# Building the expert gate table by GpSimd scatter-adds instead of one-hot products on TensorE

## The reference

```
q  = (xn @ w_pq) -> 8 heads x 2 halves x 128
s1, s2 = q @ sub_k1, q @ sub_k2            # 128 keys each
v1,i1 = top_k(s1,16); v2,i2 = top_k(s2,16) # per token and head
vs,ci = top_k(v1[:,None]+v2[None,:], 16)   # 16 of 256 pairs
e1, e2 = i1[ci // 16], i2[ci % 16]
expert = e1 * 128 + e2                     # one of 16384
gate   = softmax(vs)
out[t] = sum_k gate[t,k] * gelu(u[expert[t,k]] . xn[t]) * v[expert[t,k]]
```

## Time and profile before

| | us |
|---|---|
| median of 3 runs | 3006.87 (3006.38 to 3007.98) |
| the profiled execution | 3007.15 |
| its span, first to last instruction | 3005.4 |
| PE busy | 2962.8 (99%) |
| DVE busy | 2020.9 (67%) |
| ACT busy | 1488.6 (50%) |
| POOL busy | 169.0 (6%) |

### The profile page before, as it was taken

The page is one execution under the profiler, slowest core; times in us unless marked ns, Lnnn a source line. Parts: engine busy times, 40 slices in busy tenths (PEclk is TensorE's granted clock), DMA queues, the critical chain, the costliest instruction groups (busy, mean ns, idle before and its releaser), DMA issues.

```text
span 3005.4 us, 42961 instructions
## 1 busy us (share of the span) xinstructions
PE 2962.8 (99%) x17085; PEld 2678.9 (89%) x17085; DVE 2020.9 (67%) x2869; ACT 1488.6 (50%) x2274; POOL 169.0 (6%) x312
## 2 busy tenths in 40 slices
PE   8999999999999999999999999999999999999999
PEld 7998778888888888978789999999999999999999
DVE  5656654444445445554557988888888888888876
ACT  4355544444444444454444466447745555555553
POOL 2000000000000002140000000000010000000000
PEclk9999999999999999999999999999999999999999
DMA  7554355556554554535667779778999899899764
GB/s 255 160 169 154 114 169 193 189 188 193 184 195 182 194 189 150 169 109 208 190 208 249 237 261 338 238 222 293 337 371 360 300 328 321 310 322 318 264 221 141
DMA packets 238382, 690.73 MB, mean 230 GB/s; under 512 B 14249, under 2 KB 95177, under 8 KB 203392
## 3 DMA queue, kind: packets, MB, share of 16 engines
q1 hardware_dynamic: 221024, 598.71, 59.2%
q0 software_dynamic: 12608, 71.73, 6.3%
q10 hardware_dynamic: 4576, 17.89, 1.6%
HBM read 652.61 MB, written 33.57 MB: 228 GB/s over the span
## 4 chain that ended last, share of the span: by engine, by line
PE 51%; DVE 0%; ACTq 0%; ACT 0%; issue 0%; DVEq 0%
PE banks L2156 16%; PE banks L2232 14%; PE banks L2157 8%; PE banks L2233 7%; PE banks L2203 2%; PE banks L2253 1%; PE banks L2255 1%; PE banks L2254 1%; PE banks L2175 0%; DVE peer_features L378 0%; DVE weights_lo L195 0%; PE banks L2192 0%; PE banks L2221 0%; ACTq L2310 0%; DVE residual L2585 0%; DVE peer_scratch L2584 0%
## 5 line engine op out<-in xcount | busy, mean ns | idle before, releaser
L195 DVE TENSOR_TENSOR weights_lo<-weights,weights_hi 128x1024 fp32r<-128x1024 f32 (+4 forms) x1080 | 1228.5, 1179 | 701.8 <-ACT weights_hi L188 700.0
L188 ACT ACTIVATE weights_hi<-weights 128x1024 fp32r<-128x1024 f32 (+4 forms) x1080 | 1046.4, 1017 | 1316.8 <-PE banks L419 640.8
L2156 PE MATMUL banks<-peer_features,weights_hi 128*128 128x448 f32 (+1 forms) x2304 | 738.9, 377 | 2.7 <-DVE weights_lo L195 2.7
L417 PE MATMUL banks<-weights_hi,features_hi 128*128 128x512 f32 (+3 forms) x1600 | 605.2, 378 | 12.5 <-DVE weights_lo L195 9.3
L2157 PE MATMUL banks<-peer_features,weights_lo 128*128 128x224 f32 (+1 forms) x2304 | 615.3, 267 | 0.0
L419 PE MATMUL banks<-weights_hi,features_lo 128*128 128x512 f32 (+3 forms) x1600 | 600.5, 375 | 0.0
L418 PE MATMUL banks<-weights_lo,features_hi 128*128 128x512 f32 (+3 forms) x1600 | 600.4, 375 | 0.0
L2232 PE MATMUL banks<-peer_features,weights_hi 128*128 128x448 f32 x1568 | 492.4, 374 | 0.0
L2156 PEld LDWEIGHTS banks<-peer_features,weights_hi 128*128 128x128 f32 x2304 | 432.0, 187 | 44.2 <-DVE weights_lo L195 3.2
L2157 PEld LDWEIGHTS banks<-peer_features,weights_lo 128*128 128x128 f32 x2304 | 438.6, 190 | 0.0
L2233 PE MATMUL banks<-peer_features,weights_lo 128*128 128x224 f32 x1568 | 414.3, 264 | 0.0
(11 more groups left out here) (406 smaller groups left out, 2757.7 us busy)
## 6 DMA issues: line engine op xcount, KB each, us to landing
weights<-in_expert_u SPq DMA_DIRECT2D x128, 1024.0 KB, 5.5
weights<-in_expert_v SPq DMA_DIRECT2D x128, 1024.0 KB, 7.2
weights<-in_w_ffn_gate SPq DMA_DIRECT2D x44, 1024.0 KB, 5.1
weights<-in_w_ffn_up SPq DMA_DIRECT2D x44, 1024.0 KB, 5.1
weights<-in_w_ffn_down SPq DMA_DIRECT2D x44, 1024.0 KB, 4.8
weights<-in_w_in SPq DMA_DIRECT2D x48, 900.0 KB, 4.7
weights<-in_w_out SPq DMA_DIRECT2D x32, 1024.0 KB, 5.1
weights<-in_w_in SPq DMA_DIRECT2D x24, 704.0 KB, 4.2
```

The source lines that it names most:

```text
L188: act.activation(hi[:, k, n], raw[:, k, n], ACT.Copy).then_inc(self.hi_ready, 1 + skip)
L195: last = dve.tensor_tensor(lo[:, k, n], raw[:, k, n], hi[:, k, n].bitcast(F32), ALU.subtract)
L417: pe.matmul(out, xh, wh, start=first, stop=False)
L2156: pe.matmul(self.bank(n % 3, 2 * (T - lo)), wh[:, k, :], F[:, k, :, lo:T], start=(k == 0), stop=False)
```

## The change

1. PE's one-hot products, the transposes for them and all work of ACT and DVE for them are gone. `expert_gates` is laid out `(key, expert, token)`, is set to zero by 16 POOL DMAs of 896 KB in the feed-forward of block 1, and is filled by 256 indirect DMAs of POOL that add: each takes one slot (of 128) for all tokens of a tile, 96 or 128 values of 4 bytes, each to its own cell. DVE works out the cell numbers (two small operations a part). At the first slot of each head (every 16) POOL waits until all scatters before have landed, since two heads can name one cell.
2. The 32 row tokens are now the last 32 of the last tile, so that tile is chosen first: `RET` is (44, 10), choosing runs from step 10 to 43 and 44 to 77. The score products stand four steps ahead of each part (`SCORE`).
3. POOL's order is fixed: 160 scatters (`early`), with row gathers 0 to 2 behind the first three; then row gather c, four scatters, row gather c+1, four scatters and so on, until the scatters run out behind gather 26. Each scatter of a part waits for that part's gates (`chosen`), each gather for its buffer (`row_summed`).
4. `SUM` is now 78 to 125 without multiples of 6, 126 to 141, 143 to 150.
5. From step 2 to 271 `weights_lo` is one operation of 128x2048, that starts when both halves of `weights_hi` are there.
6. SP waits for all 256 scatters where it waited for the stored gates. The `expert_gates` loads are contiguous.

```diff
+    def split_lo_whole(self, dve, stream, i, j, half):
+        hi, lo, raw = ...
+        dve.wait_ge(self.hi_ready, i * 16 + (2 * (2 * (self.fills + j) + half) + 2))
+        dve.tensor_tensor(lo, raw, hi.bitcast(F32), ALU.subtract).then_inc(self.lo_ready, 1)
...
+                        self.pool_chain.on(pool)(pool.memset(zeros[:, :], 0.0))
+                        parts = NKEYS // self.ZEROED
+                        for n in range(parts):
+                            pool.wait_ge(ring.used, ring.done(1 + n // 2, 4 * (n % 2)))
+                            pool.dma_start(self.g_d[:, self.ZEROED * n:self.ZEROED * (n + 1), :],
+                                           zeros[:, :].rearrange("p (e t) -> p e t", e=self.ZEROED)).then_inc(self.gates_zeroed, 16)
...
-        SC, RET, TURN = 18, (22, 74), (55, 107)
-        HOT = [(58 + i, 0, ROWS // 8 + i) for i in range(16 - ROWS // 8)] + [(110 + i, 1, i) for i in range(16)]
-        SUM = [56, 57, *range(58, 74), *range(108, 142), *range(V0 - 1, V0 + 8), *range(V0 + 9, V0 + 12)]
+        FIRST, RET = NT - 1, (44, 10)
+        SUM = [s for s in range(78, 126) if s % 6] + [*range(126, 142), *range(V0 - 1, V0 + 7)]
+        SCORE = [RET[(FIRST + q // 4) % NT] + 8 * (q % 4) - 4 for q in range(4 * NT)]
...
+                    ch(dve.tensor_scalar(vif[:, 0:2, :].rearrange("p h k -> p (h k)"), eg[:, 0, slots], float(DENSE), token[:, t:t + 1],
+                                         ALU.mult, ALU.add))
+                    ch(dve.scalar_tensor_tensor(out=cell_of[:, t, slots], in0=eg[:, 1, slots], scalar=float(NKEYS * DENSE),
+                                                in1=vif[:, 0:2, :].rearrange("p h k -> p (h k)"), op0=ALU.mult, op1=ALU.add))
...
-                                for b in range(2):
-                                    sp.wait_ge(gates_out[b], 8 * BLKS)
-                                sp.wait_ge(gated, DENSE // 4)
+                                sp.wait_ge(scattered, 16 * NT * SLOTS)
...
+                    def scatter(n):
+                        t, slot = (FIRST + n // SLOTS) % NT, n % SLOTS
+                        tokens = P - ROWS if t == FIRST else P
+                        if slot % TOPK == 0:
+                            pool.wait_ge(chosen, n // (HP * TOPK) + 1)
+                            if slot > 0:
+                                pool.wait_ge(scattered, 16 * n)
+                        pool.indirect_dma_start(out=g_rows[:, :], in_=gates_of[0:tokens, t, slot:slot + 1], in_offset=None,
+                                                compute_op=ALU.add,
+                                                out_offset=bass.IndirectOffsetOnAxis(ap=cell_of[0:tokens, t, slot:slot + 1], axis=0))\
+                            .then_inc(scattered, 16)
+                    pool.wait_ge(zeroed, 16 * NKEYS // self.ZEROED)
+                    early, mixed = SLOTS + HP * TOPK, 4
+                    for n in range(early):
+                        scatter(n)
+                        if n < BUFS:
+                            gather(n)
+                    for c in range(BUFS, 2 * ROWS):
+                        gather(c)
+                        for n in range(early + mixed * (c - BUFS), min(early + mixed * (c - BUFS + 1), NT * SLOTS)):
+                            scatter(n)
...
-                        for t, r, place_in_order in hot_step(n):
-                            for g in (2 * r, 2 * r + 1):
...
-                                for c in range(4):
-                                    last = pe.matmul(self.bank(3 + g % 2, P, c * P), h[:, 0, c, :], h[:, 1, c, :],
-                                                     start=True, stop=True)
...
-                        ring.split_lo(dve, tiles, i, j, half)
+                        if s < 2:
+                            ring.split_lo(dve, tiles, i, j, half)
+                        else:
+                            ring.split_lo_whole(dve, tiles, i, j, half)
```

More of the change, by code:

```diff
@@ L196, in split_lo @@
         last.then_inc(self.lo_ready, 1 + skip)
+    def split_lo_whole(self, dve, stream, i, j, half):
+        hi, lo, raw = self.piece(self.hi, half, stream), self.piece(self.lo, half, stream), self.raw(j, half, stream)
+        dve.wait_ge(self.hi_ready, i * 16 + (2 * (2 * (self.fills + j) + half) + 2))
+        dve.tensor_tensor(lo, raw, hi.bitcast(F32), ALU.subtract).then_inc(self.lo_ready, 1)
     def wait(self, pe, i, j, half):
@@ L1927, in peer @@
             skT = scratch[:, 4096:6144].rearrange("p (j n) -> p j n", j=PQ_TILES)
-            gblk = scratch[:, 0:4096].rearrange("p (b e t) -> p b e t", b=2, t=BLK)
-            hot = [x.rearrange("p (g w c e) -> p g w c e", g=2, w=2, c=4) for x in (XN[:, 0, :], scratch[:, 4096:6144])]
             s_in = [XN[:, 1 - b, 0:8 * DENSE].rearrange("p (e t) -> p e t", t=DENSE) for b in range(2)]
-            g_in = [scratch[:, b * 2048:b * 2048 + 8 * DENSE].rearrange("p (b e t) -> p b e t", b=BLKS, t=BLK) for b in range(2)]
+            g_in = [scratch[:, b * 2048:b * 2048 + 8 * DENSE].rearrange("p (e t) -> p e t", t=DENSE) for b in range(2)]
             S = tmp("peer_scores", [P, 2, 2, DENSE])
@@ L1986, in peer @@
             scores_out = [self.sem(f"peer_scores_stored{b}") for b in range(2)]
-            gates_out = [self.sem(f"peer_gates_stored{b}") for b in range(2)]
             s_back = [self.sem(f"peer_scores_back{b}") for b in range(2)]
@@ L2127, in _, with gather @@
                     pool.sem_inc(counted, 1)
+                    self.pool_chain.on(pool)(pool.iota(token_i[:, :], pattern=[[P, NT]], base=0, channel_multiplier=1))
+                    self.pool_chain.on(pool)(pool.tensor_copy(token[:, :], token_i[:, :]))
+                    pool.sem_inc(counted, 1)
                     self.rstd_of_tiles(pool, D)
-                    for c in range(2 * ROWS):
+                    def gather(c):
                         if c % 8 == 0 and c < ROWS:
@@ L2297, in spill_sums @@
                     def spill_sums(act, span):
-                        at, cols = (ROWS, slice(T, T + DENSE)) if span < SPANS - 2 else (0, slice(DENSE, 2 * DENSE + ROWS))
+                        n = DENSE if span < SPANS - 2 else T
                         if span > 0:
@@ L2305, in spill_sums @@
                                 act.wait_ge(ring.used, piece_done(V0 + 8 * span + 7))
-                            act.activation(spill[:, c, at:T], self.psum[:, c * BANK + cols.start:c * BANK + cols.stop], ACT.Copy)\
+                            act.activation(spill[:, c, 0:n], self.bank(c, n, T), ACT.Copy)\
                                 .then_inc(spilled, 1)
@@ L2464, in leave_sums @@
                             dve.wait_ge(spilled, CHUNKS * span + c + 1)
-                            dve.tensor_tensor(spill[:, c, ROWS:T], self.bank(c, DENSE), spill[:, c, ROWS:T], ALU.add).then_inc(left, 1)
+                            dve.tensor_tensor(spill[:, c, 0:DENSE], self.bank(c, DENSE), spill[:, c, 0:DENSE], ALU.add).then_inc(left, 1)
                     def add_sums(dve, span):
                         pieces = [(4 * (span % 2), 4)] if span < SPANS - 1 else [(4 + j, 1) for j in range(4)]
-                        start = 0 if span >= SPANS - 2 else ROWS
+                        n_tokens = T if span >= SPANS - 2 else DENSE
                         for j, n in pieces:
@@ L2472, in add_sums @@
                             dve.wait_ge(left, CHUNKS * span + c + 2 * n)
-                            to = XT[:, j:j + n, :, start:T]
-                            dve.tensor_tensor(to, to, spill[:, c:c + 2 * n, start:T].rearrange("p (j i) t -> p j i t", i=2), ALU.add)\
+                            to = XT[:, j:j + n, :, 0:n_tokens]
+                            dve.tensor_tensor(to, to, spill[:, c:c + 2 * n, 0:n_tokens].rearrange("p (j i) t -> p j i t", i=2), ALU.add)\
                                 .then_inc(added, 1)
@@ L2681, in run @@
             self.turn_split_close(range(KD))
+        dense = T - self.ROWS
+        self.g_rows = nc.dram_tensor("expert_gates", (P * NKEYS * dense, 1), F32, kind="Internal").ap()
+        self.g_d = self.g_rows.rearrange("(p e t) o -> p e (t o)", e=NKEYS, t=dense)
+        self.gates_zeroed = self.sem("expert_gates_zeroed")
         self.ffn((s_up, s_down), s_in2)
```

156 lines of the change are left out of this document (44 added, 112 removed).

## The result

The kernel after took **3096.89 us** (median of 4 runs, 3093.27 to 3098.9) against 3007.29 us before (3006.38 to 3007.98): a ratio of 1.0297, 95% interval 1.0279 to 1.0315. The prediction was 2979 us, from 2954 to 3050. The change costs 90 us where 28 were to be gained. The profiled execution has a span of 3092.3 us and took 3094.99.

A forecast was written before the change was run, and what follows sets the result against it. PE, busy 99% of the span, was taken to bound the kernel: 3007.15 - 50.8 (PE) + 1 (`weights_lo`) + 19 (row 3) + 3 (SP) = 2979.4, given as 2979 us, range 2954 to 3050.

The forecast's parts named there:

- What PE loses, -50.8 us: PE: 28 one-hot steps at 1.79 us each give 50.1, two sets of transposes 0.7; score products only moved.
- `weights_lo` whole, +1 (0 to 5): DVE's one later-starting operation leaves 0.4 us slack a step; only steps 10, 133 and 142 lengthen: +1 us.
- Zeros at 0: Feed-forward: 14.7 MB more writes bring DMA share from 0.59 to about 0.7, at no cost.
- The hold: POOL: an indirect DMA starting under a DVE operation on two SBUF operands waits for its end, done 0.82 us later.
- 2.0 us a scatter: POOL's queue: three scatters a step, priced from the gather's 0.94 us; bounds 1.25 and 2.55, break-even 1.85.
- SP's wait: Before the first gate load SP waits for all scatters, delaying weight loads: +3 us, bounds 0 and 8.
- The landing term, 0.2 a scatter: POOL: every 16th scatter waits up to 4 us for a landing, +0.2 us each.
- Stall at row 3: Step 86: DVE, and so PE, waits for gather 3 behind POOL's late queue: 19 us.
- Rival B: Two scatters a step at 2.55 us, stalls of 71 at row 3 and 33 at later rows: 3064 us; chance 0.20.
- Rival A: POOL in time, scatter at most 1.85 us, no stall at row 3: 2957 to 2963 us; chance 0.20.
- Rival C: Lock works both ways, a scatter also holds DVE, some 0.4 us a step for 110 steps: 3024 us; chance 0.07.
- Rival D: 28672 additions of 4 bytes clog the DMA engines and weights come late: anything above 2990 us; chance 0.05.

The follow-up runs named there:

- e3: The changed kernel without its 256 scatter-adds, so the table stays zero; 2962.75 us, ratio 0.985.
- e4: The kernel before with `weights_lo` in one 128x2048 operation from step 2 on, nothing else changed; 3012.64 us, ratio 1.0015.
- e1: The changed kernel with `weights_lo` again in two 128x1024 operations; 3036.09 us, ratio 1.0096.
- e2: The changed kernel with `weights_lo` in four 128x512 operations, the first two after the first half of `weights_hi`; 3012.53 us, ratio 1.0014.
- e11: The changed kernel with scatters that write, the addition left out; 2976.27 us, one run.
- e8: e7 with `weights_lo` in eight 128x256 operations; 2992.91 us, ratio 0.9948.
- e14: e12 with all scatters written without the addition; 2964.5 us, one run.
- e12: e9 with the first head of each token tile written without the addition, and gather 27 ahead of POOL's last landing wait; 3002.35 us, ratio 0.9981.
- e7: e2 with gather 3 behind 136 scatters, then five a gather, POOL issuing the first gate load, first four gate products one step later; 3008.27 us.
- e5: The changed kernel with gather 3 behind 112 scatters instead of 160, then six a gather instead of four; 3104.07 us, ratio 1.0309.
- e9: e8 with the two token tiles' scatters in turns by head, a semaphore per tile, gathers near head borders moved onto them; 2983.38 us, ratio 0.9916.

## Why the prediction was wrong

**What PE loses, -50.8 us: right.** Step by step, e3 against before, the 28 one-hot steps give 50.1 us and the two sets of transposes 0.6. The score products are moved, as it said: two of them now lengthen steps 6 and 14 by 0.7 and 0.8 us, six the u steps by 0.8 each, and so the w_pq steps are longer and the u steps shorter. That e3 gains 45.2 and not 50.8 is the whole `weights_lo`. The L2203 rows are gone. "All u steps at 5.01" was too strict: the six with score products take 5.83, and eight from 76 to 97 take 5.37, as before.

**`weights_lo` whole, +1 (0 to 5): 4.65 in e4, 4.6 by steps in e3,** at the top of its bounds. What the sum looked at came as it said (step 10 +0.7, steps 133 to 143 +0.5 in all); the 3.3 that it left out are in the value steps.

**Zeros at 0: no cost seen.** The zeros are written before step 0, which begins at 1466.4 to 1470.9 us in the profiles with them and at 1466.2 and 1469.3 in the two without (before, e4).

**The hold: right.** That a scatter which starts under `weights_lo` waits for its end, and one that starts ahead of it doesn't, was read from the earlier trace rows and is what the trace after shows. e1 and e2 price it.

**2.0 us a scatter: the step that failed.** It took an unheld scatter for a gather of the earlier trace rows, 0.94 us; it is 1.41 for 96 indices and 1.55 for 128. So the room after `weights_lo` ends holds two scatters and not three, as the prediction wrote beside its bound of 2.55: "the third is lost as soon as a scatter is 0.2 us dearer than a gather". It was 0.5 to 0.6 dearer. Measured up to step 86: one POOL instruction in 2.64 us, where 2.0 was forecast and 2.55 was the upper bound (the 2.56 of the later expectations is two in a step of 5.11, without landings). e11 tests the term: at the gather's price POOL needs 1.95 us each and the same kernel takes 2976 us, against 2979 predicted. That the two are so near is partly luck: row 3 costs 11 us there (19 forecast), SP's wait and what follows 4 (3), the whole `weights_lo` 4.65 (1). The landing term, 0.2 a scatter, was sound for the kernel after (35.2 / 256 = 0.14) and a little small without a long stall (68.5 / 256 = 0.27 in e8).

**Stall at row 3: +19 forecast, 93.3 measured; later rows 0, measured 17; SP's wait +3 (0 to 8), measured 23.3.** The first two follow from the price of a scatter, but for some 2 us of the clock behind the stall. The third too: POOL is also late at its end, and SP's wait stands ahead of weight loads, so that POOL's lateness becomes PE's at once.

**Rival B (3064, 0.20)** was the mechanism and still 33 us short: its 71 at row 3 counted 41 left at 1.5, where 46 scatters at 1.86 were left (the price of the addition is paid in the stall too), and it gave SP 3 us and the whole `weights_lo` 1; its 33 for later rows was too much. The sentence that spoke for it, that an add reads its target too, got 0.20; the nearest row, an indirect DMA without addition, got the rest. The upper bound of 2.55 was taken for an extreme, and was about the value.

**Rival A** (POOL in time, 2957 to 2963) is what e3 shows, and nearly e14; both leave out the additions. **Rival C** (the lock holds DVE, 3024) falls: `weights_lo` takes at most 2.36 us over 270, 91 of which began inside a scatter, and where DVE stands waiting for `weights_hi` it starts 0.03 us after it (median) whether a scatter runs or not. By the Trainium skill, SBUF — State Buffer, "SBUF: two separate sides", the pair belongs to whoever starts first and the other is fully blocked; the trace agrees for POOL, where 91 of 93 scatters waited, and shows no such wait for DVE behind an indirect DMA. **Rival D** (DMA clog): the 3097 us are not from it, as e1 and e2 show, which make the same additions in 61 and 84 us less; e12's slow steps are the one sign of something like it.

## What to carry to other kernels

Don't price a DMA with an addition by one without: bound it by twice (here it was 1.5 to 1.6 times), ask how many fit between two of the operations that hold it, and take the count just below seriously. An operation of DVE on two SBUF operands made longer is paid above all by POOL: where POOL's queue is full, many short ones beat one long one (one of 2.29 us cut into four of 0.69: 84 us here; four into eight of 0.42: 15 more, e7 to e8). In a queue in order, put an early-wanted transfer where its buffer comes free, neither behind a batch nor in front of a full buffer; but moving it doesn't help while the queue lacks capacity (e5). And price a long stall of PE with what its clock costs behind it, 2 to 3 us here.

## What the runs showed of the hardware

- An indirect scatter with addition occupies POOL 1.41 us for 96 indices and 1.55 for 128; without addition 0.92 and 0.97; a gather of 128 rows 0.98. Between two 0.30.
- It is held if it starts under a DVE operation on two SBUF operands, and ends 1.28 to 1.46 us after that operation does; DVE is not held by it. Operations that begin inside it don't hold it: with eight of 128x256 back to back the mean is 1.60 us.
- 14 waits for landings of scatters took 35.2 us of POOL in the kernel after, some of them in the stall, and 68.5 us (longest 10.4) in e8.
- PE's granted clock was 0.50 while PE stood, and for 4 to 6 us of work behind a stall of 93 and one of 20 us.
- Unexplained: where the first head's scatters were plain and the later ones added, four steps with all queues slow cost 24 us in e12; with all of them plain (e14) or all adding (e9) there were none.
